# A second attention whose score products go two heads at a time, on 64 rows each, with the gate sums as a product of their own

## What is computed

```python
log_f = jax.nn.log_sigmoid(f_logit.astype(jnp.float32) + b_forget[l].astype(jnp.float32))
cum = jnp.cumsum(log_f, axis=1).transpose(0, 2, 1)
...
def block_attention(q, k, v, scale, diag_mask, cum=None):
    for q0 in range(0, S, Q_BLOCK):
        q1 = q0 + Q_BLOCK
        s = jnp.einsum('bhqd,bhkd->bhqk', q[:, :, q0:q1], k[:, :, :q1]).astype(jnp.float32) * scale
        if cum is not None:
            s = s + cum[:, :, q0:q1, None] - cum[:, :, None, :q1]
        mask = jnp.concatenate([jnp.ones((Q_BLOCK, q0), dtype=bool), diag_mask], axis=1)
        s = jnp.where(mask, s, -jnp.inf)
        p = jax.nn.softmax(s, axis=-1).astype(v.dtype)
        outs.append(jnp.einsum('bhqk,bhkd->bhqd', p, v[:, :, :q1]))
```

## Time and profile before

| | |
|---|---|
| runs | 1750.52, 1748.83, 1750.08 us; median 1750.08 |
| profiled execution | 1749.1 us, its span 1747.3 us |
| PE busy | 1720.7 us (98%) |
| DVE, ACT, POOL busy | 1092.4, 681.1, 195.6 us |
| clock granted to TensorE | 0.998 of full speed, mean |
| score products (L1481) | 256 records, 91.1 us busy; mask products 64 records, 14.1 us |
| value products (L1533) | four widths, 64 records each: 17.3, 13.0, 9.6 and 6.2 us busy |

### The profile page before, as it was taken

The page is one execution under the profiler, slowest core; times in us unless marked ns, Lnnn a source line. Parts: engine busy times, 40 slices in busy tenths (PEclk is TensorE's granted clock), DMA queues, the critical chain, the costliest instruction groups (busy, mean ns, idle before and its releaser), DMA issues.

```text
span 1747.3 us, 21946 instructions
## 1 busy us (share of the span) xinstructions
PE 1720.7 (98%) x7794; PEld 1371.4 (78%) x7794; DVE 1092.4 (63%) x1652; ACT 681.1 (39%) x1122; POOL 195.6 (11%) x136
## 2 busy tenths in 40 slices
PE   9999999999999999999999999999999999999997
PEld 7777777877888888888878677777788888888886
DVE  6999886866545555542359988867755555555222
ACT  5645444334343222222235454542533422222222
POOL 1720100010020000001144210000101100000010
PEclk9999999999999999999999999999999999999999
DMA  6342120333433333333332412113333333333331
GB/s 163 83 101 61 49 61 25 102 86 90 119 97 91 97 97 98 96 90 100 84 96 65 106 51 55 49 43 103 91 96 108 97 96 96 96 96 93 95 92 69
DMA packets 309940, 152.19 MB, mean 87 GB/s; under 512 B 30372, under 2 KB 309150, under 8 KB 309868
## 3 DMA queue, kind: packets, MB, share of 16 engines
q1 hardware_dynamic: 309560, 150.99, 31.1%
q10 hardware_dynamic: 308, 0.25, 0.1%
HBM read 149.09 MB, written 2.10 MB: 87 GB/s over the span
## 4 chain that ended last, share of the span: by engine, by line
PE 91%; DVE 6%; ACT 1%; issue 1%; DMA 1%; SPq 0%; ACTq 0%; DVEq 0%; POOLq 0%
PE bank L1421 70%; PE bank L1500 12%; PE bank L1481 4%; PE bank L1533 2%; PE bank L1512 2%; DVE w_lo L987 2%; DVE k_t L1271 1%; DVE c_acc L1047 1%; DMA raw<-in_w_in 1%; PE bank L1444 0%; ACT w_hi L659 0%; DVE tmp L1008 0%; DVE c_acc L1313 0%; DVE c_acc L1306 0%; DVE ln_std L1300 0%
## 5 line engine op out<-in xcount | busy, mean ns | idle before, releaser
L659 ACT CAST w_hi<-raw 128x1024 fp32r<-128x1024 f32 (+4 forms) x330 | 301.3, 916 | 755.1 <-PE bank L1421 746.5
L987 DVE TENSOR_TENSOR w_lo<-raw,w_hi 128x1024 fp32r<-128x1024 f32 (+4 forms) x330 | 355.8, 1081 | 221.0 <-ACT w_hi L659 219.8
L1421 PE MATMUL bank<-h_hi,w_hi 128*128 128x512 f32 (+1 forms) x1200 | 473.9, 395 | 6.6 <-DVE w_lo L987 6.2
L1421 PE MATMUL bank<-h_hi,w_lo 128*128 128x512 f32 (+1 forms) x1200 | 467.4, 390 | 0.0
L1421 PE MATMUL bank<-h_lo,w_hi 128*128 128x512 f32 (+1 forms) x1200 | 467.3, 389 | 0.0
L1421 PEld LDWEIGHTS bank<-h_hi,w_hi 128*128 128x128 f32 (+1 forms) x1200 | 224.5, 187 | 63.9 <-issue 8.2
L1008 DVE TENSOR_TENSOR tmp<-bank,rstd_x 128x512 f32<-128x512 f32 x140 | 96.7, 690 | 268.0 <-PE bank L1421 259.1
L1421 PEld LDWEIGHTS bank<-h_lo,w_hi 128*128 128x128 f32 (+1 forms) x1200 | 224.6, 187 | 48.7 <-issue 2.7
L1421 PEld LDWEIGHTS bank<-h_hi,w_lo 128*128 128x128 f32 (+1 forms) x1200 | 224.5, 187 | 48.1
L1047 DVE SCALAR_TENSOR_TENSOR c_acc<-u_pad,dwk_l,c_acc 128x512 f32<-128x512 f32 x240 | 178.6, 765 | 1.2
L547 POOL TENSOR_TENSOR x_acc<-x_acc,x_sq 128x512 f32<-128x512 f32 x31 | 53.5, 1726 | 868.4 <-ACT x_sq L669 536.1
(11 more groups left out here) (228 smaller groups left out, 2138.3 us busy)
## 6 DMA issues: line engine op xcount, KB each, us to landing
raw<-in_w_in SPq DMA_DIRECT2D x96, 512.0 KB, 3.8
raw<-in_w_ffn_gate SPq DMA_DIRECT2D x44, 512.0 KB, 3.8
raw<-in_w_ffn_up SPq DMA_DIRECT2D x44, 512.0 KB, 3.8
raw<-in_w_ffn_down SPq DMA_DIRECT2D x32, 512.0 KB, 3.8
raw<-in_w_out SPq DMA_DIRECT2D x16, 512.0 KB, 3.8
raw<-in_w_ffn_down SPq DMA_DIRECT2D x16, 384.0 KB, 3.3
raw<-in_w_bo_a SPq DMA_DIRECT2D x16, 256.0 KB, 2.8
raw<-in_w_bo_b SPq DMA_DIRECT2D x16, 256.0 KB, 2.7
```

What stands on the lines that cost most here:

```text
L659: last = nc.scalar.copy(to, of)
L987: last = nc.vector.tensor_tensor(to, of, part.bitcast(F32), ALU.subtract)
L1421: ins = nc.tensor.matmul(bank_t[0:rows, :], wt[slot][:, w], x, start=first and k == 0 and p == 0, stop=last and k == k_tiles - 1 and p == 2)
```

## The change

The order of the steps in branch B is now given by FOX_ORDER: head, query block and place in `p_b` for each of a pair's eight steps, with the two heads of a query block next to each other (blocks 0, 3, 1, 2). `fox_logits` makes both steps' scores at once: two products of 64 rows, head 0 from rows 0 to 63 and head 1 from rows 64 to 127 of the same tile, into two banks; then two products of 40 rows that add the gate sums; then the two masks. It is called for even g, in the step before (g - 1), so that the scores of an even step come one step later than before, and those of an odd one when they did.

The gate sums are an operand `cum_x`, with the 8 heads' sums rounded to the f32r type at rows 0 and 64 and up, and what the rounding left at rows 32 and 96 and up, all else 0; the other operand, `head_of`, is 1 on the rows of one head. GpSimd builds both behind the rotary sums: in layer 0 it first clears `cum_x` and makes `head_col`. Nothing is put in row 64 of `q_t` and `k_t` any more, so the ones, their semaphore, SP's four loads and their waits go. `f_sum` now lies under the end of `p_t`, so that TensorE's transposes of step 7 wait for GpSimd's last product of the chain. Queries and keys of a pair are put out in one piece of 128 partitions. VectorE normalises step g - 1 ahead of the maximum of step g where g is even and in branch B.

The diff, cut to its core:

```diff
 P_AT = (0, P, 3 * P, 6 * P)
+FOX_ORDER = ((0, 0, 0), (1, 0, P), (0, 3, 2 * P), (1, 3, 6 * P), (0, 1, 0), (1, 1, 2 * P), (0, 2, 4 * P), (1, 2, 7 * P))
+CUM_ROWS = 32 + HEADS
 P_T_STEP = 3 * P
...
     return [(to[:, 0:size], of[:, 0:size])]
+def step_of(g):
+    pair, s = g // 8, g % 8
+    return (pair, s // 4, s % 4, P_AT[s % 4]) if pair < PAIRS else (pair, *FOX_ORDER[s])
...
     rstd_col = sb("rstd_col", [P, TT])
-    f_sum = sb("f_sum", [P, T])
+    cum_x = sb("cum_x", [P, T], F32R)
+    head_col = sb("head_col", [P, 32])
...
     misc_t = at("misc_t", r0 + 82 * KB, [P, T])
+    f_sum = at("f_sum", r0 + 88 * KB, [P, T])
+    head_of = at("head_of", tmp_off + 6 * KB, [P, PAIRS, P], F32R)
     key_a = at("key_a", r0 + 84 * KB, [P, T])
...
-            def keys(l, pair):
-                sp.wait_ge(cum_ready, l + 1)
-                sp.wait_ge(score_done, l * STEPS + 8 * (pair + 1))
-                sp.dma_start(k_t[NOPE:NOPE + 1, 2 * pair:2 * pair + 2, :],
-                             f_sum[2 * ROPE + 2 * pair:2 * ROPE + 2 * pair + 2, :]).then_inc(cum_put[pair], 16)
             w_in, w_out, w_gate, w_up, w_down = (dram[k] for k in ("w_in", "w_out", "w_ffn_gate", "w_ffn_up", "w_ffn_down"))
...
                                             rope_t[rows, g // 4 * 2 + 1, :], ALU.add).then_inc(rope_put, 1)
+                pool.wait_ge(rope_put, HEADS * (l + 1))
+                if l == 0:
+                    nc.gpsimd.tensor_scalar(cum_x[:], ident[:].unsqueeze(1).broadcast_to([P, TT, P]), 0.0, None, ALU.mult).then_inc(cum_zero, 1)
+                    pool.wait_ge(cum_zero, 1)
+                    nc.gpsimd.memset(head_col[:, 0:PAIRS], 0.0).then_inc(cum_zero, 1)
+                    pool.wait_ge(cum_zero, 2)
+                    for n in range(4):
+                        first = 32 * n + n // 2
+                        nc.gpsimd.tensor_copy(head_col[32 * n:32 * n + HEADS, 0:PAIRS],
+                                              ident[32 * n:32 * n + HEADS, first:first + HEADS:2]).then_inc(cum_zero, 1)
+                        pool.wait_ge(cum_zero, 3 + n)
+                pool.wait_ge(cum_ready, l + 1)
+                passed(pool)
+                for e in range(2):
+                    nc.gpsimd.tensor_copy(cum_x[64 * e:64 * e + HEADS, :], f_sum[F, :]).then_inc(cum_hi, 1)
+                    pool.wait_ge(cum_hi, 2 * l + 1 + e)
+                nc.gpsimd.tensor_copy(head_of[:], head_col[:, 0:PAIRS].unsqueeze(2).broadcast_to([P, PAIRS, P])).then_inc(cum_put, 1)
+                pool.wait_ge(cum_put, 3 * l + 1)
+                for e in range(2):
+                    nc.gpsimd.tensor_tensor(cum_x[64 * e + 32:64 * e + CUM_ROWS, :], f_sum[F, :], cum_x[64:64 + HEADS, :].bitcast(F32),
+                                            ALU.subtract).then_inc(cum_put, 1)
+                    pool.wait_ge(cum_put, 3 * l + 2 + e)
                 evac.add(12)
                 for pair in range(2 * PAIRS):
-                    if pair < PAIRS:
-                        pool.wait_ge(score_done, score.add(8))
-                        passed(pool)
-                        nc.gpsimd.memset(q_t[NOPE:NOPE + 1, 2 * pair:2 * pair + 2, :], 1.0).then_inc(ones_put, 1)
-                        pool.wait_ge(ones_put, op.add())
                     if pair:
...
                 pair_low(2 * PAIRS - 1)
-                score.add(STEPS // 2)
                 pool.wait_ge(pv_done, pv.add(HEADS))
...
-                    q = g % 4
+                    n = g % 4
+                    _, _, q, p_at = step_of(g)
                     dve.wait_ge(exp_done, ex.add())
-                    mine(nc.vector.reciprocal(row_inv[:, q:q + 1], row_sum[:, q:q + 1]))
-                    p = p_b[:, P_AT[q]:P_AT[q] + (q + 1) * P]
-                    nc.vector.tensor_scalar(p, p, row_inv[:, q:q + 1], None, ALU.mult).then_inc(norm_done, 1)
+                    mine(nc.vector.reciprocal(row_inv[:, n:n + 1], row_sum[:, n:n + 1]))
+                    p = p_b[:, p_at:p_at + (q + 1) * P]
+                    nc.vector.tensor_scalar(p, p, row_inv[:, n:n + 1], None, ALU.mult).then_inc(norm_done, 1)
...
                         evacuated(nc.vector.tensor_tensor(tmp[pair % 2][:], from_bank[:], rstd_x[:], ALU.mult))
+                    elif kind == "q":
+                        evacuated(nc.vector.scalar_tensor_tensor(q_t[:, 2 * pair, :], from_bank[:], FOX_SCALE, rstd_x[:], ALU.mult, ALU.mult))
                     else:
-                        for e in range(2):
-                            rows = slice(NOPE * e, NOPE * (e + 1))
-                            if kind == "q":
-                                ins = nc.vector.scalar_tensor_tensor(q_t[0:NOPE, 2 * pair + e, :], from_bank[rows, :], FOX_SCALE,
-                                                                     rstd_x[rows, :], ALU.mult, ALU.mult)
-                            else:
-                                ins = nc.vector.tensor_tensor(k_t[0:NOPE, 2 * pair + e, :], from_bank[rows, :], rstd_x[rows, :], ALU.mult)
-                        evacuated(ins)
+                        evacuated(nc.vector.tensor_tensor(k_t[:, 2 * pair, :], from_bank[:], rstd_x[:], ALU.mult))
                 for g in range(STEPS):
+                    n, pair, q = g % 4, g // 8, step_of(g)[2]
+                    norm_first = pair >= PAIRS and g % 2 == 0
+                    if norm_first:
+                        normalise(g - 1)
                     dve.wait_ge(score_done, score.add())
-                    q = g % 4
-                    nc.vector.tensor_reduce(neg_max[:, q:q + 1], s_bank[score_slot(g)][:, 0:(q + 1) * P], AX_X, ALU.max,
+                    nc.vector.tensor_reduce(neg_max[:, n:n + 1], s_bank[score_slot(g)][:, 0:(q + 1) * P], AX_X, ALU.max,
                                             negate=True).then_inc(max_ready, 1)
-                    if g:
+                    if g and not norm_first:
                         normalise(g - 1)
...
-                def logits(g):
-                    pair, s = g // 8, g % 8
-                    e, q = s // 4, s % 4
-                    kind, head = pair // PAIRS, 2 * (pair % PAIRS) + e
-                    if g % 8 == 0 and kind == 1:
-                        pe.wait_ge(evac_done, fed + FEED.index(f"k{pair % PAIRS}") + 1)
-                        pe.wait_ge(ones_put, op.add())
-                        pe.wait_ge(cum_put[pair % PAIRS], 16 * (l + 1))
-                    rows = (NOPE + ROPE + TT, NOPE + 1)[kind]
+                def latent_logits(g):
+                    _, e, q, _ = step_of(g)
+                    head, rows, w = 2 * (g // 8) + e, NOPE + ROPE + TT, (q + 1) * P
+                    pe.wait_ge(exp_done, ex.add())
+                    nc.tensor.matmul(s_bank[score_slot(g)][:, 0:w], q_t[0:rows, head, q * P:w], k_t[0:rows, head, 0:w],
+                                     start=True, stop=True).then_inc(score_done, 1)
+                def fox_logits(g):
+                    pair, q = g // 8 - PAIRS, step_of(g)[2]
+                    if g % 8 == 0:
+                        pe.wait_ge(evac_done, fed + FEED.index(f"k{pair}") + 1)
+                    ex.add()
                     pe.wait_ge(exp_done, ex.add())
                     w = (q + 1) * P
-                    b = s_bank[score_slot(g)]
-                    ins = nc.tensor.matmul(b[:, 0:w], q_t[0:rows, head, q * P:w], k_t[0:rows, head, 0:w], start=True, stop=True)
-                    if kind == 1:
-                        ins = nc.tensor.matmul(b[:, q * P:w], ident_b[:], mask_b[:], start=False, stop=True, skip_group_check=True)
-                    ins.then_inc(score_done, 1)
+                    b = [s_bank[score_slot(g + e)] for e in range(2)]
+                    for e in range(2):
+                        rows = slice(NOPE * e, NOPE * (e + 1))
+                        nc.tensor.matmul(b[e][:, 0:w], q_t[rows, 2 * pair, q * P:w], k_t[rows, 2 * pair, 0:w], start=True, stop=True)
+                    for e in range(2):
+                        rows = slice(64 * e, 64 * e + CUM_ROWS)
+                        nc.tensor.matmul(b[e][:, 0:w], head_of[rows, pair, :], cum_x[rows, 0:w], start=False, stop=True, skip_group_check=True)
+                    for e in range(2):
+                        nc.tensor.matmul(b[e][:, q * P:w], ident_b[:], mask_b[:], start=False, stop=True,
+                                         skip_group_check=True).then_inc(score_done, 1)
+                def logits(g):
+                    if g < STEPS // 2:
+                        latent_logits(g)
+                    elif g % 2:
+                        fox_logits(g - 1)
...
                 def turn(g):
-                    q = g % 4
+                    _, _, q, p_at = step_of(g)
+                    if g == 7:
+                        pe.wait_ge(cum_put, 3 * (l + 1))
                     pe.wait_ge(norm_done, nm.add())
...
                     for k in range(q + 1):
-                        at_k = P_AT[q] + k * P
```

(1 more changed line is left out.)

29 lines of the change are left out of this document (13 added, 16 removed).

## The result

The changed kernel takes 1758.58 us in the median of five runs (1758.44 to 1760.71), the kernel before 1750.08. The ratio is 1.0054, with a 95% interval of 1.0042 to 1.0065. So it is slower, by some 9 us, and the time lies above the predicted range.

The account below looks back on a forecast made before the run. The prediction took TensorE's stream to bound the kernel (91% of the chain of waits). Its terms, -4.7 + 3.5 + 0.3 = -0.9 us, gave 1749.2 us against a median of 1750.08, no change that can be told; range 1744 to 1756.

Parts of the forecast that it names:

- TensorE's stream: Branch B's scores on TensorE: paired 64-row products plus gate sums save 0.59 us per pair of heads, 4.7 us in all.
- the chain: GpSimd's gate-sum work behind the rotary sums delays VectorE in the first steps: 3.5 us more, between 0 and 9.3.
- VectorE's order: Normalising the step before first in branch B cuts the margin before the transposes: 0.3 us more, between 0 and 2.
- rival 2: Each chain step gets in ahead of VectorE through the port lock, delaying steps 0 to 2: 1754.7 us; chance 0.2.
- the group: A two-step group in branch B at 512 columns on TensorE: 0.47 fixed plus 0.86 plus 0.23, so 1.56 us.
- the sums: Gate-sum products in branch B: one pass over the same columns for both heads, 0.63 us per pair of heads.
- Rival 3: Branch B's 64-row products run one after the other, so scores and sums are paid twice: 1771 us; chance 0.05.
- Late normalises: In branch B, normalises may come too late for TensorE's transposes: 0.3 us more, between 0 and 2.
- The wait ahead of step 7's transposes: TensorE's new wait for GpSimd's chain costs nothing unless the chain takes over 16 us.
- the first three marks: Pairs starting within 0.01 us; groups costing about 0.47 us plus products; the stretch from step 32 shorter by 2.3 a layer.
- the fourth: Steps 0 to 3 longer by 1 to 2.5 us, with VectorE's normalise named as ending TensorE's idle time.

Follow-up runs that it names:

- fastest version: The changed kernel with head_col behind the region, GpSimd's chain held until the sixth scores, and six layer-0 operations made behind the masks: 1744.41 us.
- a_home: The changed kernel with the 128-byte tile head_col put behind the 91-KB region instead of ahead of it: 1749.11 us.

## Why the prediction was wrong

**The step that failed is one that isn't there.** The sum, -4.7 + 3.5 + 0.3, has terms for TensorE's stream, the chain and VectorE's order, and so takes the pace of all products outside the attention part as unchanged, without a reason given. The diff has a line that changes it: `head_col` is allocated ahead of r0, and moves 91 KB of tiles by 128 bytes. The prediction gives it no price. The 2,172 products that stream from these tiles then took 6 ns more each. It is worth 9.5 us (1758.6 against 1749.1), more than any term of the sum. No rival had it either; the time that rival 2 would have given, 1754.7, has another mechanism and doesn't reach it.

**The terms that are there** are read on the kernel with the tile behind the region, whose time is 1749.11 where the prediction gives 1749.2. That agreement is partly luck. The terms as measured add up to +0.1 and not to -0.9; what makes up for it is the base of the sum, 1750.08, the median of three executions, where twenty later ones of the same kernel have 1749.26. Term by term:

- *TensorE's stream, -4.7:* branch B is 2.28 us shorter a layer (110.69 to 108.41), -4.6 in all. Right, and by its parts: in all 32 groups the two heads' products start 6 or 7 ns apart (209.890 and 209.897 in the changed kernel's layer 0), the group costs 1.57 for 1.56, the sums 0.55 for 0.63. Rival 3 falls with the run of the heads one after the other.
- *The chain, +3.5 (0 to 9.3):* +4.74, 2.69 in layer 0 and 2.05 in layer 1. The mechanism is shown by moving the chain alone, late and early. It was sized 1.2 us too low. VectorE operations with a single tile operand suffer too: two first taps took 2.25 us for 1.00 where the subtractions of 125.97 to 128.71 began beside them, and a normalise 0.70 for 0.35, ending just behind the second subtraction (128.86). Of SBUF's shared port pair, the Trainium skill says under "SBUF: two separate sides" (SBUF — State Buffer) that VectorE takes part with two SBUF inputs or in a two-port mode; the tap and the normalise have one tile operand each, and the rows don't name the mode in which they ran. Their lengths fit the second case: with the chain late and GpSimd idle when they start, a normalise takes 0.29, 0.35, 0.42 and 0.48 us for 128 to 512 columns, so 0.06 per 128 columns, where the maximum takes 0.13 (0.28 for 128 columns, 0.68 for 512).
- *Late normalises, +0.3 (0 to 2):* nothing. TensorE is never idle in steps 32 to 63 of the changed kernel or of this one. In the fastest version, which has the same order on VectorE, TensorE is idle ahead of all its transposes for 0.3 us together, less than the 0.5 of before.
- *The wait ahead of step 7's transposes, 0:* right; no idle time of TensorE stands there.

Of "What would show it", the first three marks came, and the fourth nearly: from the first scores to the start of step 4's work it is 2.7 and 2.0 us longer with the tile behind the region (3.2 and 1.0 in the changed kernel) where 1 to 2.5 was forecast, with a normalise named as what ended the idle time. They were marks of the terms; none looked outside the attention part, which is why all could come true and the time be wrong.

**The clock** had no term. A stretch at half clock is 3.4 us long and costs from 0.5 us (the second one above) to 1.8 (the first score product starts at 121.96 with the chain late, 120.18 in a_home, whose profile has none), and one just ahead of the first scores is in eight of the sixteen profiles of this case, of kernels with and without the change. Window 116.6 to 119.9, the kernel before and the one with the late chain:

```profile
116.60:119.90 3.30, 3.30 (x15) 2.51 (x14) 1.40 (x2) 2.45 (x4) 2.08 (x2) 1.00 0.47 137
```

```profile
116.60:119.90 3.30, 3.30 (x9) 2.59 (x10) 0.88 (x1) 1.63 (x2) 2.21 (x2) 0.55 0.51 147
```

Fifteen products fall in the one, nine in the other. That fits how the times of one kernel fall in two heaps: with the late chain five executions took 1744.6 to 1744.9, all at a mean granted clock of 0.998, and five 1746.0 to 1746.4, four of them at 0.997. Where in the span the clock dropped is on record only for the profiled ones. What makes the grant fall in one execution and not in the next stays open; the idle times ahead of it (0.45, 0.45 and 1.05) are the same.

## What to carry to other kernels

A diff that allocates a tile moves every tile behind it: write down the addresses before and after, modulo 256, of every operand of the products that fill the time, and check that moving operand and weights agree. If nothing else explains a small loss, compare the mean duration of products that the change does not touch. And an engine with free time is not free at any moment: GpSimd's chain (118.8 to 128.7 in layer 0) cost 4.7 us in all beside steps where VectorE sets the pace, and 0.35 ten microseconds later.
